# The second layer of the second feed-forward: seven products of block sums in place of eight block products

## The reference

```
hm = rms_norm_2(x, norm_mlp[l]) @ mlp_w1[l]        # (256,1024) @ (1024,4096)
x = x + jnp.square(jax.nn.relu(hm)) @ mlp_w2[l]    # (256,4096) @ (4096,1024)
```

## Time and profile before

| | |
|---|---|
| median of three runs | 844.53 us |
| the profiled execution, its own time | 844.23 us |
| its span, first to last instruction | 842.3 us |
| granted TensorE clock, mean | 1.000 |
| TensorE busy | 826.9 us (98%) |
| VectorE busy | 581.4 us (69%) |
| ScalarE busy | 429.3 us (51%) |
| GpSimd busy | 126.6 us (15%) |

### The profile page before, as it was taken

One profiled execution on the slowest core, in us unless ns is written; L12 is line 12 of the kernel. 1 busy time (PEld: TensorE's weight loads), 2 busy tenths in 40 slices (PEclk: granted clock), 3 DMA queues, 4 the chain that ended last, 5 costly groups with the idle time before them and its releaser, 6 DMA issues.

```text
span 842.3 us, 13156 instructions
## 1 busy us (share of the span) xinstructions
PE 826.9 (98%) x5366; PEld 706.0 (84%) x5366; DVE 581.4 (69%) x861; ACT 429.3 (51%) x637; POOL 126.6 (15%) x163
## 2 busy tenths in 40 slices
PE   9999999999999999999999999999999999999998
PEld 7988867898888888888868899888788888888886
DVE  4479784637467977777764999985757577666662
ACT  4366733463447756655554577354444355444440
POOL 0146000210010000000020999610010000000000
PEclk9999999999999999999999999999999999999999
DMA  9975434352445765556514525101424367655521
GB/s 308 320 231 202 173 138 164 126 200 101 149 150 180 246 216 184 184 173 215 178 50 140 182 90 196 52 10 44 126 84 140 101 201 263 234 179 180 193 101 51
DMA packets 92631, 135.89 MB, mean 161 GB/s; under 512 B 4467, under 2 KB 76795, under 8 KB 92444
## 3 DMA queue, kind: packets, MB, share of 16 engines
q1 hardware_dynamic: 90572, 129.72, 46.1%
q10 hardware_dynamic: 1264, 2.70, 1.0%
q0 software_dynamic: 736, 2.63, 0.9%
HBM read 133.46 MB, written 1.06 MB: 160 GB/s over the span
## 4 chain that ended last, share of the span: by engine, by line
PE 77%; DVE 15%; ACT 3%; DMA 2%; issue 2%; POOL 1%; SPq 0%; DVEq 0%; ACTq 0%
PE acc L2295 25%; PE work L2320 16%; PE work L2295 11%; PE work L2322 8%; PE work L2264 3%; DVE arena L1789 2%; DVE split_extra_slot L1498 2%; PE work L2234 2%; DVE split_operands L1498 2%; DVE arena L1812 2%; PE work L2202 1%; PE work L2966 1%; PE work L2648 1%; PE work L2288 1%; PE work L2667 1%
## 5 line engine op out<-in xcount | busy, mean ns | idle before, releaser
L1498 DVE TENSOR_TENSOR split_operands<-weight_ring,split_operands 128x2048 fp32r<-128x2048 f32 x74 | 170.0, 2302 | 70.8 <-ACT split_operands L959 70.5
L2295 PE MATMUL acc<-split_operands 128*128 128x512 f32 x808 | 193.0, 391 | 0.2 <-DVE split_operands L2173 0.2
L2295 PEld LDWEIGHTS acc<-split_operands 128*128 128x128 f32 x808 | 149.9, 188 | 32.5 <-issue 0.6
L959 ACT ACTIVATE split_operands<-weight_ring 128x2048 fp32r<-128x2048 f32 x74 | 140.9, 1909 | 66.4 <-PE acc L2295 23.9
L2320 PE MATMUL work<-split_operands 128*128 128x512 f32 x400 | 142.0, 398 | 0.0
L2322 PE MATMUL work<-split_operands 128*128 128x256 f32 x400 | 112.3, 281 | 0.0
L1498 DVE TENSOR_TENSOR split_extra_slot<-weight_ring,split_extra_slot 128x2048 fp32r<-128x2048 f32 x34 | 79.0, 2323 | 23.6 <-ACT split_extra_slot L959 23.4
L2320 PEld LDWEIGHTS work<-split_operands 128*128 128x128 f32 x400 | 75.2, 188 | 18.5
L2295 PE MATMUL work<-split_operands 128*128 128x256 f32 x640 | 82.9, 285 | 0.6 <-DVE split_operands L1498 0.5
L946 ACT ACTIVATE arena<-work 128x512 f32<-128x512 f32 (+3 forms) x81 | 37.7, 473 | 89.3 <-PE work L2322 33.9
L2295 PEld LDWEIGHTS work<-split_operands 128*128 128x128 f32 x640 | 78.8, 192 | 4.3 <-issue 4.0
(11 more groups left out here) (351 smaller groups left out, 1167.2 us busy)
## 6 DMA issues: line engine op xcount, KB each, us to landing
weight_ring<-in_mlp_w SPq DMA_DIRECT2D x32, 1024.0 KB, 5.2
weight_ring<-in_w_up SPq DMA_DIRECT2D x22, 1024.0 KB, 5.1
weight_ring<-in_w_in SPq DMA_DIRECT2D x20, 1024.0 KB, 6.0
weight_ring<-in_w_down SPq DMA_DIRECT2D x11, 1024.0 KB, 4.9
weight_ring<-in_w_out SPq DMA_DIRECT2D x8, 1024.0 KB, 4.9
weight_ring<-in_w_mk SPq DMA_DIRECT2D x4, 1024.0 KB, 5.0
weight_ring<-in_w_mv SPq DMA_DIRECT2D x4, 1024.0 KB, 4.9
weight_ring<-in_w_mq SPq DMA_DIRECT2D x4, 1024.0 KB, 5.2
```

The lines of the kernel that those rows point to most:

```text
L959: act.activation(slot_of(u)[:, 0, :], weights(u, 2048), ACT.Copy).then_inc(high_ready, 1)
L1498: dve.tensor_tensor(slot[:, 1, :], weights(split_units[i], 2048), slot[:, 0, :], ALU.subtract).then_inc(low_ready, 1)
L2295: ins = pe.matmul(out, lhs(p), rhs(q), start=(start and n == 0), stop=(stop and n == 2))
```

## The change

The sixteen units of the second layer are taken as seven pairs (unit s with unit s + 7) and two single ones. For a pair, the activations form a matrix of 2 x 2 blocks (two token tiles by two units), the weights one too (two units by two halves of the output columns). The eight block products become seven products of sums of blocks. GpSimd makes four weight sums of 1024 elements (`weight_sum`) and four activation sums of 256 elements (`rows_summed`) per pair. ScalarE and VectorE split, per pair, seven factor weights of 1024 elements, three of them raw blocks and four of them sums, in place of two whole units of 2048, and five groups of activation rows (four of 256 elements, one of 768). Each of the seven products has a bank of its own (four `acc`, three `work`) in which it is added up over all pairs; the fourth `work` bank serves the hidden units. Hence from the fifth hidden unit on these are computed with three products of 256 columns per block, and ScalarE drains them with the ReLU. At the end VectorE adds the seven banks to the residual in eight additions, while TensorE multiplies the last two units in the old way into four banks. The ring slot of a weight unit of a pair is free when its factors are split and its sums are made. The seven factor weights have one slot each, and each is filled again for the next pair when its product is done.

```
-MLP_LAG = 2
+MLP_PAIRS = MLP_UNITS // 2 - 1
+MLP_ORDER = tuple(k // 2 + MLP_PAIRS * (k % 2) for k in range(2 * MLP_PAIRS)) + (MLP_UNITS - 2, MLP_UNITS - 1)
+AHEAD = 4
+FACTORS = (1, 2, 3, 5, 7, 6, 4)
+FIRST_FACTORS = 3
...
-    for j in range(MLP_UNITS + MLP_LAG):
-        if j < MLP_UNITS:
-            units.append(("m1", j))
-        if j >= MLP_LAG:
-            units.append(("m2", j - MLP_LAG))
+    units += [("m1", j) for j in MLP_ORDER[:AHEAD]]
+    for n in range(MLP_PAIRS):
+        units += [("m2", n), ("m2", n + MLP_PAIRS)]
+        units += [("m1", j) for j in MLP_ORDER[AHEAD + 2 * n:AHEAD + 2 * n + 2]]
+    units += [("m2", j) for j in MLP_ORDER[-2:]]
...
-                  (("out2", "xq", "xwo", "m1", "m2"), (None, 12352, 8192, 20480)))
+                  (("out2", "xq", "xwo"), (None, 12352, 8192, 20480)), (("m1", "m2"), (20480,) + MLP_UNITS * (None, 8192)))
...
+        t_sums = {n: v[:, 4 * i:4 * i + 4, :].rearrange("p (k a) t -> p k (a t)", k=2)
+                  for n, v, i in ((1, hT, 0), (3, hT, 1), (2, mixT, 0), (4, mixT, 1))}
+        factor_at = {1: 12288, 2: 14336, 3: 16384, 4: 18432, 6: 20480, 7: 22528, 5: 24576}
+        factor_w = {n: cut_split(at, 2, 2, 512) for n, at in factor_at.items()}
+        factor_rows = {1: (early_rows, 0), 2: (early_rows, 1), 3: (early_rows, 2),
+                       5: (late_rows, 0), 6: (late_rows, 1), 7: (late_rows, 2), 4: (late_rows, 3)}
+        last_rows = cut_split(factor_at[1], 2, 2, 2, SEQ)
...
+        hidden_bank = bank(("m1_half", MLP_ORDER[AHEAD - 1], 1))
+        factor_bank = {2: acc(("m2", 0)), 3: acc(("m2", 1)), 4: acc(("m2", 2)), 1: acc(("m2", 3))}
+        factor_tile = {5: ("m1_half", MLP_ORDER[AHEAD - 2], 0), 7: ("m1_half", MLP_ORDER[AHEAD - 2], 1),
+                       6: ("m1_half", MLP_ORDER[AHEAD - 1], 0)}
+        factor_bank.update({n: bank(name) for n, name in factor_tile.items()})
+        def factor(s, n):
+            return len(FACTORS) * s + FACTORS.index(n)
+        def raw_block(s, row, col):
+            return weights(("m2", s + MLP_PAIRS * row), 2, D)[:, :, 512 * col:512 * col + 512]
+        def factor_source(s, n):
+            if n <= FIRST_FACTORS:
+                return raw_block(s, int(n > 1), int(n == 3))
+            return t_sums[{5: 1, 7: 3, 6: 2, 4: 4}[n]]
...
+        ROW_STEPS = (("early", 0, 1), ("early", 1, 2), ("early", 2, 3), ("late", 0, 6), ("late", 3, 4))
...
+                    if held in in_sums:
+                        n, row = held[1] % MLP_PAIRS, held[1] // MLP_PAIRS
+                        sp.wait_ge(factor_low, factor(n, 3 if row else 1) + 1)
+                        sp.wait_ge(weight_sums, t_sum(n, 4 if row else 3))
+                    else:
+                        sp.wait_ge(*((low_ready, SPLIT[held] + 1) if held in SPLIT else LAST_OF_UNIT[held]))
...
+            def weight_sum(s, n):
+                if s:
+                    pool.wait_ge(factor_low, factor(s - 1, {1: 5, 3: 7, 2: 6, 4: 4}[n]) + 1)
+                plus, minus = {1: (raw_block(s, 0, 1), raw_block(s, 0, 0)), 3: (raw_block(s, 1, 1), raw_block(s, 0, 1)),
+                               2: (raw_block(s, 1, 1), t_sums[1]), 4: (raw_block(s, 1, 0), t_sums[2])}[n]
+                pool.tensor_tensor(t_sums[n], plus, minus, ALU.subtract).then_inc(weight_sums, 1)
+            def rows_summed(s):
+                pool.wait_ge(relu_full, 2 * s + 1)
+                if s:
+                    pool.wait_ge(rows_low, 5 * (s - 1) + 4)
+                a11, a21 = activation_block(s, 0, 0), activation_block(s, 1, 0)
+                pool.tensor_tensor(s_rows[:, 2], a11, a21, ALU.subtract).then_inc(row_sums, 1)
+                pool.wait_ge(relu_full, 2 * s + 2)
+                pool.tensor_tensor(s_rows[:, 0], a21, activation_block(s, 1, 1), ALU.add).then_inc(row_sums, 1)
+                pool.wait_ge(row_sums, 4 * s + 2)
+                pool.tensor_tensor(s_rows[:, 1], s_rows[:, 0], a11, ALU.subtract).then_inc(row_sums, 1)
+                pool.wait_ge(row_sums, 4 * s + 3)
+                pool.tensor_tensor(s_rows[:, 3], activation_block(s, 0, 1), s_rows[:, 1], ALU.subtract).then_inc(row_sums, 1)
+            pool.wait_ge(*full(("m1", 0)))
+            pool.wait_ge(*low_there(("rows", "mlp", TT - 1, 1)))
+            for s in range(MLP_PAIRS):
+                pool.wait_ge(*loaded(("m2", s)))
+                weight_sum(s, 1)
+                pool.wait_ge(*loaded(("m2", s + MLP_PAIRS)))
+                weight_sum(s, 3)
+                rows_summed(s)
+                pool.wait_ge(weight_sums, t_sum(s, 1))
+                weight_sum(s, 2)
+                pool.wait_ge(weight_sums, t_sum(s, 2))
+                weight_sum(s, 4)
...
+            def hidden_out(k):
...
+                if k >= 2:
+                    act.wait_ge(relu_full, k - 1)
+                if k == 0:
+                    drain(name, hidden[0], halves(name), ACT.Relu).then_inc(reader(name), 1)
                 else:
-                    if j >= 3:
-                        for c in range(2):
-                            act.wait_ge(*drained(("m1_half", j - 2, c)))
-                    for c in range(2):
-                        drain(("m1_half", j, c), low_half[j % 2][:, c, :], bank(("m1_half", j, c))[:, SEQ:512]
-                              ).then_inc(low_halves, 1)
-                act.wait_ge(relu_full, j + 1)
-                if j >= 3:
-                    act.wait_ge(unit_spent, SPENT[("m2", j - 3)])
-                act.activation(relu2_s[j % 3][:, 0], relu2[j % 2], ACT.Copy).then_inc(relu_high, 1)
-                high_parts(before(("m1", j + 1)) + 3)
-            high_parts(len(split_units) - 1)
+                    act.wait_ge(m1_full, k - AHEAD + 1)
+                    act.activation(hidden[k % 2], hidden_bank[:, :].rearrange("p (c t) -> p c t", c=2), ACT.Relu
+                                   ).then_inc(m1_read, 1)
+            def factor_highs(s, numbers):
+                for n in numbers:
+                    if s:
+                        act.wait_ge(factor_done, factor(s - 1, n) + 1)
+                    elif n in (6, 7):
+                        act.wait_ge(*LAST_OF_UNIT[("m1", MLP_ORDER[1])])
+                    if n <= FIRST_FACTORS:
+                        act.wait_ge(*loaded(("m2", s + MLP_PAIRS * int(n > 1))))
+                    else:
+                        act.wait_ge(weight_sums, t_sum(s, T_OF[n]))
+                    act.activation(factor_w[n][:, 0], factor_source(s, n), ACT.Copy).then_inc(factor_high, 1)
+            def row_highs(s, steps):
+                for i in steps:
+                    if s:
+                        act.wait_ge(factor_done, factor(s - 1, ROW_STEPS[i][2]) + 1)
+                    if i in (2, 3):
+                        act.wait_ge(row_sums, 4 * s + 4)
+                    else:
+                        act.wait_ge(relu_full, 2 * s + 1 + int(i > 0))
+                    high, _, src = row_step(s, i)
+                    act.activation(high, src, ACT.Copy).then_inc(rows_high, 1)
...
+            for s in range(1, MLP_PAIRS):
+                factor_highs(s, FACTORS[:FIRST_FACTORS])
+                row_highs(s, (0, 1, 2))
+                hidden_out(2 * s + 2)
+                high_parts(upto(later[2 * s - 2]))
+                factor_highs(s, FACTORS[FIRST_FACTORS:])
+                row_highs(s, (3, 4))
+                hidden_out(2 * s + 3)
+                high_parts(upto(later[2 * s - 1]))
+            act.wait_ge(factor_done, factor(MLP_PAIRS - 1, 1) + 1)
...
+            def factor_lows(s, numbers):
+                for n in numbers:
+                    dve.wait_ge(factor_high, factor(s, n) + 1)
+                    dve.tensor_tensor(factor_w[n][:, 1], factor_source(s, n), factor_w[n][:, 0], ALU.subtract
+                                      ).then_inc(factor_low, 1)
+            def row_lows(s, steps):
+                for i in steps:
+                    dve.wait_ge(rows_high, 5 * s + i + 1)
+                    high, low, src = row_step(s, i)
+                    dve.tensor_tensor(low, src, high, ALU.subtract).then_inc(rows_low, 1)
...
+            dve.wait_ge(copied_6, 1)
+            link(dve.tensor_tensor(partial[0], factor_bank[1][:, :], low_half.rearrange("p c t -> p (c t)"), ALU.add))
+            link(dve.tensor_tensor(partial[1], factor_bank[7][:, :], partial[0], ALU.add))
+            link(dve.tensor_tensor(result(0, 0), factor_bank[1][:, :], result(0, 0), ALU.add))
+            link(dve.tensor_tensor(result(0, 1), factor_bank[5][:, :], result(0, 1), ALU.add))
+            link(dve.tensor_tensor(result(0, 1), partial[0], result(0, 1), ALU.add))
+            link(dve.tensor_tensor(result(1, 0), partial[1], result(1, 0), ALU.add))
+            link(dve.tensor_tensor(result(1, 1), factor_bank[5][:, :], result(1, 1), ALU.add))
+            link(dve.tensor_tensor(result(1, 1), partial[1], result(1, 1), ALU.add))
...
+            def hidden_unit(k):
+                unit = ("m1", MLP_ORDER[k])
```

(30 more changed lines are left out.)

188 lines of the change are left out of this document (137 added, 51 removed).

## The result

The changed kernel takes 887.64 us (median of 4 runs, 886.04 to 891.38) against 844.56 (843.78 to 845.20) of the kernel before, run beside it: ratio 1.0517, interval 1.0495 to 1.0539. It is 43 us slower where 17.5 were forecast, and it lies outside the range (838 to 880). The direction was right, the size wrong. The profiled execution took 886.04 us, its span 884.3; all times within an execution are from it.

The account below looks back on a forecast made before the run. VectorE, held up by GpSimd's sums, was to pace the changed stage: 16.5 + 7.5 = 24.0 us per pair. TensorE's end at 713.4 + 6T, +18.3 on the profiled 844.23, gave 862 us named; range 838 to 880.

Parts of the forecast that it names:

- TensorE's balance: TensorE in the second layer: 9.6 us saved by fewer products, 1.4 lost on hidden units, -8.1 us in all.
- VectorE alone: VectorE's own work per pair of units, without GpSimd's interference: 16.5 us against 13.6 before.
- The price of the sums: Time VectorE loses per pair to GpSimd's eight sums: taken as 7.5 us, between 5.3 and 9.0.
- upper bound of 9.0: Most that a pair's sums cost VectorE: 4 x 1.8 + 4 x 0.45 = 9.0 us, period 25.5.
- Start-up: Start of the paired stage: fifth product's rows ready near 697, where TensorE wants them at 693.2; costs 3.8 us.
- Three to four more for the sums: Microseconds that GpSimd's sums add to some 21 us of VectorE and ScalarE work before the first fifth product.
- End hidden: After the last pair, VectorE's eight adds (about 6.3 us) lie beside TensorE's last 10.9 us: nothing gained or lost.
- rival 4: GpSimd's own loop of sums, load and waits is the bound, slower still: 875 to 890 us, chance 0.16.
- threshold of 1.1 us: GpSimd's loop decides once its waiting per sum passes 1.1 us, worked out as (25 - 15.7)/8.
- Rival 1: TensorE stays the bound, GpSimd's sums falling mostly where VectorE waits: 836 to 840 us, chance 0.15.
- The signs named ahead: Expected profile: VectorE above 90%, factor weights 1.2 to 3 us, sums of 1024 2.5 to 3, TensorE idle 2 to 4.
- A pair every 24 us: Expected steady period of a pair of units in the second layer, set by VectorE: 24 us.

Follow-up runs that it names:

- experiment 1: Changed kernel with GpSimd's eight sums per pair cut to 4 columns of each row, all waits and other instructions kept: 846.3 us, ratio 1.0018.
- experiment 5: Changed kernel, early hidden units drained and squared sooner at the start: first order 885.77 us, the second form 887.38; the second form with sums cut to 4 columns 837.51.
- experiment 6: Changed kernel with VectorE making all sums, row sums first, ScalarE's drain earlier, ScalarE squaring later hidden units, and the second form's start: 846.97 us, ratio 1.0021.
- experiment 2: Kernel before the change, with three GpSimd sums of 1024 elements that nobody reads added behind each of 14 hidden units: 882.96 us, ratio 1.0450.
- the second form: Changed kernel, at the start hidden unit 1 drained and squared ahead of all factors, 2 behind the first, 3 ahead of the last four: 887.38 us, ratio 1.0499.
- experiment 4: Changed kernel with only GpSimd's four row sums of 256 elements cut to 4 columns, the sums of 1024 whole: 874.37 us, ratio 1.0338.

## Why the prediction was wrong in size

The forecast put the end of TensorE's work at 713.4 + 6 x 24.0 = 857.4; it ended at 881.1. The 23.7 us between are 10.8 at the start (rows of the fifth product at 707.8, 697 forecast), 12.6 in six rounds (156.6 instead of 144: five of 26.8 and one of 22.4), and 0.2 at the end. The forecast took all six rounds as whole ones; in the last of them GpSimd has no weight sums left, which hid about 4 us of the error. The median lies 1.6 us above the profiled execution, which makes up the rest.

- **TensorE's balance, -8.1 us: right.** The round of 21.1 us stands in experiments 1, 5 and 6 (21.08), and the kernel with small sums of experiment 5, where nothing else is late, takes 837.5 us where 836.1 were worked out.
- **VectorE alone, 16.5 us: a little high.** The spacing of its rows in experiment 5 gives 15.9 (1024 elements 1.13 to 1.17 with the gap, 1.18 taken).
- **The price of the sums, 7.5 us a round: the step that failed.** It measured 11.0, above even the upper bound of 9.0. The mechanism was named rightly: whoever has started keeps the other out. The size failed twice. A sum of 1024 was drawn out to 1.84 us from sums of 256 and 512; the shortest here takes 2.39 and VectorE pays 2.2. With 1.8 instead of 2.21 for each large sum and 0.45 instead of 0.54 for each small one, the eight came out 2.0 us too cheap. And 1.5 us were taken off for overlaps and for sums that fall where VectorE is idle or reads PSUM. Both places exist (0.56 us in experiment 2, the adds at 693.00), but the steady round has neither: VectorE is never idle there and reads no PSUM. With the measured price for the large sums and 0.54 for the small ones the same sum gives 16.5 + 11.0 = 27.5, with VectorE's true 15.9 it gives 26.9. (The Trainium skill, "GPSIMD Engine Reference", section "3. Performance versus the Vector engine", has 4497 ns for 2048 fp32 elements; half of it, an estimate, is 2.25 us. The trace agrees, with 2.39 for the shortest sum and a price of 2.2, where the prediction followed its own slope of 1.84.)
- **Start-up, 3.8 us: failed by the same term.** "Three to four more for the sums" were 12.5 in this order (from the low half at 666.00 to the rows 41.8 us, 29.3 in experiment 1) and 13.5 in the second form (experiment 5): by 707.7 us six weight sums, two of them for the next pair, and the row sums have been made beside VectorE's first round. A further 1.7 us came from the weights' landing at 673.5 instead of 671.8: the load was issued 1.4 us later, for a reason ahead of this stage that was not followed, and took 0.3 longer. The two long waits of TensorE at VectorE's adds, 9.9 and 7.2 us, are the most striking rows of the profile and weren't foreseen, but they cost nothing while VectorE is the bound: in experiment 5 both are gone, others of 6.6 and 4.6 us stand elsewhere, and the time is the same. Only with the sums small do such waits, 4.1 and 3.1 us there, and the half clock behind them cost 9 us.
- **End hidden: right.** 16.6 us from the start of the last fifth product to the end, 16.4 forecast.
- **The rivals.** The time lies in rival 4's interval (875 to 890), but not by its mechanism: GpSimd is idle a third of the time, the chain that ended last runs over VectorE, and the round follows VectorE's price (experiment 4). (Its threshold of 1.1 us comes to 1.2 by its own sum; nothing hangs on it.) Rival 1 needed VectorE to have slack for it; 5.2 us a round were there and 11.0 were asked.

The signs named ahead held in the main: VectorE full, factor weights between 1.2 and 3.4 us, sums of 1024 at 2.4 to 3.4, TensorE waiting some 3 to 4 us a pair before the fifth product and a hidden unit. "A pair every 24 us" did not.

## What to carry to other kernels

Before moving elementwise work of two SBUF inputs to GpSimd beside a VectorE that works on SBUF, add nearly its whole duration to VectorE's busy time (here 2.2 us for sums whose shortest took 2.39); take off only what falls in VectorE's waits or its reads of PSUM. If VectorE then passes the bounding engine, GpSimd's help costs more than VectorE's own doing (here 2.2 against 1.2 us for 1024 elements). Time an operation at the size in question, or take the nearest larger figure; a line through two small sizes of GpSimd gave 1.84 us for what takes 2.39 at least.

## What the runs showed of the hardware

- A VectorE instruction held up by GpSimd is recorded as busy: the same low half of 1024 elements is 1.2 or 3.4 us long. "Busy 30.00 of 30" therefore doesn't say that VectorE computes all the time; for 11 us of each 26.8 it was held. ScalarE wasn't touched: its copies of 2048 elements are 1.91 us before and after.
- VectorE's adds with one input in PSUM weren't held: 0.74 us for two, beside a sum (693.00 us) and without one of 1024 (708.07). The two that met a sum in experiment 2 (683.91 and 694.35 us) took 0.74 as well.
- TensorE ran in part at its lower level, 1.2 GHz, after a wait: the hidden unit behind the wait of 4.05 us in experiment 1 took 8.12 us, 5.92 elsewhere, and the granted clock at its start was 0.50. In the changed kernel the granted clock was 0.80 on average from 690 to 720 us, where TensorE had waited 9.9 us, and 1.00 in the next 30, where it was busy for 29.4. Such a stretch added 2.2 us (8.12 - 5.92) and 2.6 us (6.84 - 4.27, experiment 6) to a wait of 4. It doesn't follow every wait: in the changed kernel the hidden unit behind 2.88 us at 770.46 took 7.52 us, the one behind 2.86 us at 850.73 took 6.02.
- Sums of 1024 on GpSimd take 2.4 to 3.4 us beside a working VectorE. Three in a row beside low halves of 2048 take 3.25 each (9.76 in experiment 2), so GpSimd, too, is held.
